# Stick breaking by pairs of heads, gate jobs spread over the linear attention's scan, and a stage of four branch splits dissolved

## What is computed

```python
# branch 2: stick breaking, 8 heads of 64, by blocks of 128 queries
z = einsum("bhqd,bhkd->bhqk", q * 64 ** -0.5, k)
log_keep = where(strict, log_sigmoid(-z), 0)
between = cumsum(log_keep, axis=3, reverse=True) - log_keep
weights = where(strict, exp(log_sigmoid(z) + between), 0)
y_c = einsum("bhqk,bhkd->bhqd", weights, v)
# branch 3: gated linear attention, 4 heads of 128, chunks of 16 tokens
#   o = q_dec @ state + (causal q_dec k_inv^T) @ v;  state = state * g_last + k_dec^T @ v
y_d = rms_norm(o) * silu(gate)
# merge
gates = sigmoid(x @ w_merge)                   # 4 x 1024 columns
merged = sum(gates[n] * (y[n] @ w_branch[n]) for n in range(4))
out = merged @ w_out
```

## Time and profile before

| | us |
|---|---|
| runs | 1879.58, 1874.11, 1877.41 |
| median | 1877.41 |
| profiled execution | 1880.32 |
| its span | 1878.5 |
| TensorE busy | 1638.3 (87%) |
| VectorE busy | 1237.1 (66%) |
| ScalarE busy | 826.8 (44%) |
| mean granted clock | 0.926 |

### The profile page before, as it was taken

The page is one execution under the profiler, slowest core; times in us unless marked ns, Lnnn a source line. Parts: engine busy times, 40 slices in busy tenths (PEclk is TensorE's granted clock), DMA queues, the critical chain, the costliest instruction groups (busy, mean ns, idle before and its releaser), DMA issues. The chain is left out here.

```text
span 1878.5 us, 25694 instructions
## 1 busy us (share of the span) xinstructions
PE 1638.3 (87%) x10701; PEld 1477.9 (79%) x10701; DVE 1237.1 (66%) x1389; ACT 826.8 (44%) x953; POOL 33.0 (2%) x48
## 2 busy tenths in 40 slices
PE   2899998999799997999979996887896938999994
PEld 2789887999698987999868996766785837888883
DVE  4777488778657556665455956435564747899895
ACT  1345434333334543344234562236613316777772
POOL 0100000000100000000000000000000000000000
PEclk9999999999899998999989998978887968999997
DMA  8964347898654234566265552102311336999991
GB/s 300 301 220 158 135 138 255 305 320 301 208 149 135 92 111 147 179 228 220 69 178 167 177 159 68 44 25 67 91 67 62 118 136 228 364 350 368 361 342 68
DMA packets 226041, 348.07 MB, mean 185 GB/s; under 512 B 14596, under 2 KB 156656, under 8 KB 225792
## 3 DMA queue, kind: packets, MB, share of 16 engines
q1 hardware_dynamic: 225920, 346.36, 54.9%
HBM read 345.29 MB, written 1.97 MB: 185 GB/s over the span
## 5 line engine op out<-in xcount | busy, mean ns | idle before, releaser
L457 PE MATMUL bank<-layer_split,hT_pair 128*128 128x256 f32 (+1 forms) x4224 | 513.4, 282 | 9.6 <-DVE hT_pair L314 4.6
L457 PEld LDWEIGHTS bank<-layer_split,hT_pair 128*128 128x128 f32 x4224 | 499.3, 191 | 15.7 <-issue 9.0
L184 DVE TENSOR_TENSOR layer_split<-layer_raw,layer_split 128x2048 fp32r<-128x2048 f32 x122 | 279.6, 2292 | 98.6 <-ACT layer_split L172 97.1
L172 ACT ACTIVATE layer_split<-layer_raw 128x2048 fp32r<-128x2048 f32 x122 | 233.7, 1915 | 203.6 <-PE bank L457 114.2
L184 DVE TENSOR_TENSOR expert_split<-expert_raw,expert_split 128x2048 fp32r<-128x2048 f32 x96 | 219.4, 2289 | 41.5 <-ACT expert_split L172 41.3
L172 ACT ACTIVATE expert_split<-expert_raw 128x2048 fp32r<-128x2048 f32 x96 | 184.2, 1920 | 71.5 <-PE bank L1782 39.5
L457 PE MATMUL bank<-split_w,hT_pair 128*128 128x256 f32 (+1 forms) x1248 | 179.8, 308 | 31.5 <-PEq L599 13.7
L457 PEld LDWEIGHTS bank<-split_w,hT_pair 128*128 128x128 f32 x1248 | 170.2, 204 | 42.2 <-issue 34.9
L184 DVE TENSOR_TENSOR split_w<-raw_w,split_w 128x2048 fp32r<-128x2048 f32 x52 | 119.2, 2292 | 52.8 <-ACT split_w L172 52.3
L669 PE MATMUL bank<-layer_split,ffnh_aT 128*128 128x512 f32 x528 | 127.0, 396 | 2.8 <-DVE ffnh_aT L741 2.8
L172 ACT ACTIVATE split_w<-raw_w 128x2048 fp32r<-128x2048 f32 x52 | 99.4, 1912 | 62.1 <-PE bank L457 52.8
(11 more groups left out here) (447 smaller groups left out, 1828.6 us busy)
## 6 DMA issues: line engine op xcount, KB each, us to landing
layer_raw<-in_ada_w SPq DMA_DIRECT2D x48, 1024.0 KB, 5.7
layer_raw<-in_ffn_w_gate_up SPq DMA_DIRECT2D x44, 1024.0 KB, 5.2
raw_w<-in_w_in SPq DMA_DIRECT2D x40, 1024.0 KB, 5.1
layer_raw<-in_w_in SPq DMA_DIRECT2D x38, 1024.0 KB, 6.6
expert_raw<-in_w_gate SPq DMA_DIRECT2D x32, 1024.0 KB, 7.3
expert_raw<-in_w_up SPq DMA_DIRECT2D x32, 1024.0 KB, 7.2
expert_raw<-in_w_down SPq DMA_DIRECT2D x32, 1024.0 KB, 7.0
layer_raw<-in_ffn_w_down SPq DMA_DIRECT2D x22, 1024.0 KB, 5.1
```

The costliest lines, as they stand in the source:

```text
L172: self.nc.scalar.activation(self.pair[:, j % self.pairs, 0, 0:self.size[n]], self.raw[:, n % self.depth, 0:self.size[n]], ACT.Copy).then_i ...
L184: self.nc.vector.tensor_tensor(self.pair[:, j % self.pairs, 1, 0:self.size[n]], self.raw[:, n % self.depth, 0:self.size[n]], self.pair[:, ...
L457: ins = nc.tensor.matmul(out, lhs, rhs, start=c == 0 and tp + wp == 0, stop=c == job.k - 1 and tp == 1)
```

## The change

Four edits.

1. `stick_breaking` goes over 4 pairs of heads. The buffers hold two heads (temps of twice the size), and every elementwise instruction that can do so takes both: minimum, Exp, Ln, maximum and add, the middle part of `keep`, Exp of the weights. Those that read a bank (one a head), the strict parts of `keep` and the masks are one a head, the latter over two blocks of 128 columns at once. TensorE has one gate job after the scores and one after the cumulative products of a round. The low half of a unit comes every round, ahead of `keep`.
2. `gla` gets its 12 jobs in another order over the 16 steps.
3. `gla` also splits branches 0 and 1: two ScalarE copies at steps 12 and 14 (the first waits until all gate jobs have used `hP`), two VectorE subtractions after the state scan of head 3 and two steps later.
4. The four `split_fm` calls go. `LateSplit` splits branches 2 and 3 at the head of the merge's block, and the jobs of these branches wait for it.

```diff
@@ project
+                        if job.wait is not None:
+                            pe.wait_ge(*job.wait)
@@ LateSplit
+            def wait(self, n):
+                return (self.lo_done.sem, n - 1) if n >= 2 else None
+            def scalar(self, act):
+                self.ring.hi(act, self.first)
+                for row, pair in zip(self.rows, self.pairs):
+                    signal(nc.scalar.activation(pair[:, 0, :, :].rearrange("p c s -> p (c s)"),
+                                                row[:, :, :].rearrange("p c s -> p (c s)"), ACT.Copy), self.hi_done)
+                self.ring.hi(act, self.ring.ahead(self.first, 1))
+            def vector(self, dve):
+                self.ring.lo(dve, self.first)
+                for n, (row, pair) in enumerate(zip(self.rows, self.pairs)):
+                    dve.wait_ge(self.hi_done.sem, n + 1)
+                    signal(nc.vector.tensor_tensor(pair[:, 1, :, :], row[:, :, :], pair[:, 0, :, :].bitcast(FP), ALU.subtract),
+                           self.lo_done)
+                self.ring.lo(dve, self.ring.ahead(self.first, 1))
@@ mixer
-                for n in range(4):
-                    split_fm(f"mixer_split{n}", yT[n], yP[n], 4)
+                split = LateSplit(ring, U_BR, yT[2:4], yP[2:4])
-                project("mixer_merge", ring, jobs)
+                project("mixer_merge", ring, jobs, norm=split)
@@ stick_breaking, TensorE
+                    for i in range(PAIRS + 2):
+                        if i < PAIRS:
+                            if i >= 1:
+                                pe.wait_ge(scaled.sem, 2 * i)
+                            for h in range(2):
...
+                            ins.then_inc(scored, 1)
                             beside.multiply(pe, 1)
+                        if 1 <= i <= PAIRS:
+                            n = i - 1
+                            pe.wait_ge(kept.sem, 3 * n + 3)
+                            if n >= 1:
+                                pe.wait_ge(added.sem, 2 * n)
+                            for h in range(2):
...
+                            ins.then_inc(cumed, 1)
+                            beside.multiply(pe, 1)
+                        if i >= 2:
+                            n = i - 2
+                            pe.wait_ge(masked.sem, 2 * n + 2)
...
@@ stick_breaking, VectorE
+                            for h in range(2):
+                                signal(v.tensor_tensor(wt[:, n % 2, h, :], score[:, n % 2, h, :], ps[2 + h][:, 0:Wd], ALU.add), added)
+                        ring.lo(dve, min(first + i + 1, ring.ahead(last, 1)))
+                        if i < PAIRS:
+                            dve.wait_ge(logged.sem, i + 1)
+                            kp, lg = keep[:, i % 2, :, :], ab[:, i % 2, :, :]
+                            done(dve, v.scalar_tensor_tensor(lg, score[:, i % 2, :, :], 0.0, lg, ALU.max, ALU.add), floored)
+                            for h in range(2):
+                                signal(v.scalar_tensor_tensor(ends(kp[:, h, :]), ends(lg[:, h, :]), -1.0, strict, ALU.mult, ALU.mult), kept)
+                            signal(v.tensor_scalar(kp[:, :, P:S], lg[:, :, P:S], -1.0, None, ALU.mult), kept)
@@ stick_breaking, ScalarE
+                    for i in range(PAIRS + 1):
+                        if i < PAIRS:
+                            act.wait_ge(prepped.sem, i + 1)
+                            z = ab[:, i % 2, :, :].rearrange("p h s -> p (h s)")
+                            done(act, a.activation(z, z, ACT.Exp), exped)
+                            signal(a.activation(z, z, ACT.Ln, bias=1.0), logged)
+                        if i >= 1:
+                            act.wait_ge(added.sem, 2 * i)
+                            w = wt[:, (i - 1) % 2, :, :].rearrange("p h s -> p (h s)")
+                            signal(a.activation(w, w, ACT.Exp), weighed)
+                        beside.leave(act, True, 2 * i)
+                        ring.hi(act, min(first + i + 1, ring.ahead(last, 1)))
+                        beside.leave(act, True, 2 * i + 1)
@@ gla, ScalarE
                 for h in range(4):
                     yield
+                    if h >= 2:
+                        if h == 2:
+                            act.wait_ge(ring.used, ring.uses(beside.jobs[-1].unit))
+                        signal(a.activation(hP[:, 0, 4 * (h - 2):4 * (h - 2) + 4, :].rearrange(flat),
+                                            early[h - 2][:, :, :].rearrange(flat), ACT.Copy), early_hi)
                     act.wait_ge(o_sum, h + 1)
@@ gla, VectorE, after the state scan of head h (h up to 4)
+                    if h >= 3:
+                        dve.wait_ge(early_hi.sem, h - 2)
+                        pair = hP[:, :, 4 * (h - 3):4 * (h - 3) + 4, :]
+                        signal(v.tensor_tensor(pair[:, 1, :, :], early[h - 3][:, :, :], pair[:, 0, :, :].bitcast(FP), ALU.subtract),
+                               early_lo)
                     yield
@@ gla
-            woven(ring, beside, [2, 2, 2, 2, 2, 1] + [0, 1] + [0] * 8, {"tensor": tensor, "scalar": scalar, "vector": vector})
+            woven(ring, beside, [2, 1, 1, 1, 1, 1] + [1, 1, 1, 1, 1] + [0] * 5, {"tensor": tensor, "scalar": scalar, "vector": vector})
```

More of the change, by code:

```diff
@@ L1473, in _, with __init__, tensor, gpsimd @@
                                               ps[b][:, :]).then_inc(out, 1)
+        class LateSplit:
+            def __init__(self, ring, first, rows, pairs):
+                self.ring, self.first, self.rows, self.pairs = ring, first, rows, pairs
+                self.hi_done, self.lo_done = Count(nc, "late_split_hi"), Count(nc, "late_split_lo")
+            def wait(self, n):
+                return (self.lo_done.sem, n - 1) if n >= 2 else None
+            def tensor(self, pe):
+                pass
+            def gpsimd(self, pool):
+                pass
+            def scalar(self, act):
[11 more added lines that the diff above has]
+                self.ring.lo(dve, self.ring.ahead(self.first, 1))
+            def ready(self, pe, c):
+                pass
         def second_part():
@@ new lines, in stick_breaking @@
+            Wd, PAIRS = S + P, 4
+            ab, score, keep, wt = (temps[:, i, :, :].rearrange("p b (h s) -> p b h s", h=2) for i in range(4))
+            scored, cumed, mixed = (new_sem(nc, f"sb_pe_{n}") for n in ("scored", "cumed", "mixed"))
+            scaled, prepped, floored, kept, added, masked, out = (
+                Count(nc, f"sb_dve_{n}") for n in ("scaled", "prepped", "floored", "kept", "added", "masked", "out"))
+            exped, logged, weighed = (Count(nc, f"sb_act_{n}") for n in ("exp", "log", "weights"))
@@ new lines, in stick_breaking, with ends, _ @@
+            first = beside.jobs[0].unit
+            last = beside.jobs[-1].unit
+            def ends(z):
+                return z.rearrange("p (c s) -> p c s", c=3)[:, 0:3:2, :]
+            strict = const("sb_strict").unsqueeze(1).broadcast_to([P, 2, P])
+            with nc.Block() as block:
+                @block.sync
+                def _(sp):
+                    ring.feed(sp, ring.ahead(last, 1))
+                @block.tensor
+                def _(pe):
+                    for i in range(PAIRS + 2):
[3 more added lines that the diff above has]
+                            for h in range(2):
+                                kk, qq = k[64 * h:64 * h + 64, i, :], q[64 * h:64 * h + 64, i, :]
+                                nc.tensor.matmul(ps[h][:, 0:S], kk[:, 0:P], qq, start=True, stop=True)
+                                ins = nc.tensor.matmul(ps[h][:, S:Wd], kk[:, P:S], qq[:, P:S], start=True, stop=True)
+                            ins.then_inc(scored, 1)
+                            beside.multiply(pe, 1)
+                        if 1 <= i <= PAIRS:
[4 more added lines that the diff above has]
+                            for h in range(2):
+                                kp, bank = keep[:, n % 2, h, :], ps[2 + h]
@@ L2720, in _ @@
-                    @block.scalar
-                    def _(act):
-                        for i in range(H + 1):
-                            if i < H:
-                                act.wait_ge(prepped.sem, i + 1)
-                                z = ab[:, i % 2, :]
-                                done(act, a.activation(z, z, ACT.Exp), exped)
-                                a.activation(z, z, ACT.Ln, bias=1.0).then_inc(logged.sem, 1)
-                            if i >= 1:
-                                n = i - 1
-                                act.wait_ge(added.sem, n + 1)
-                                w = wt[:, n % 2, :]
-                                a.activation(w, w, ACT.Exp).then_inc(expd.sem, 1)
-                            beside.leave(act, True, i)
-                            ring.hi(act, min(first + i // 2 + 1, first + n_beside))
-                        beside.leave(act, True, len(beside.jobs))
@@ L2739, in gla @@
```

(1 more changed line is left out.)

127 lines of the change are left out of this document (39 added, 88 removed).

## The result

| | before | after |
|---|---|---|
| median | 1876.62 (4 runs, 1874.11 to 1879.58) | 1855.35 (4 runs, 1844.37 to 1861.75) |
| ratio | | 0.9873, 95% interval 0.9845 to 0.9902 |
| profiled execution | 1880.32 (span 1878.5) | 1844.37 (span 1842.5) |

The account below looks back on a forecast made before the run. No engine fills stick breaking, linear attention or norm; TensorE's clock is partly low, and everything later waits for the mixer. Terms 2 + 11 + 4 + 8.6 - 0.2 = 25.4 us gave 1854.9 or 1852.0; 1854 named, range 1848 to 1867.

Parts of the forecast that it names:

- The sum itself: Whole kernel: gains of stick breaking, front, scan and splits, less 0.2 us, together 25.4 us.
- its two results: Whole kernel: 1854.9 us counted from the profiled execution, 1852.0 counted from the median of three runs.
- Stick breaking, forecast 69.5 us: Stick-breaking stage by pairs of heads: rounds of 15.2 us, 2 us less than 71.5; bounds -4.5 to +6.
- Rival B: Stick breaking doesn't gain, as every round pauses TensorE: stage 75 to 77 us, kernel 1860; chance 0.13.
- The front, forecast 11.0 us earlier: Linear attention up to first state products: fewer jobs ahead, so these start 11.0 us earlier; bounds 9 to 12.
- The scan, forecast 37.1 us: First state products to last output: 4 us less than 41.1, with TensorE the bound at the high clock.
- rival A: Scan: TensorE falls to 1.2 GHz again behind the last gate job, 6.4 us back, kernel 1860; chance 0.19.
- The bound for this term: Scan: 63 us if all its jobs, updates and outputs run at the low clock.
- the prediction's own sign: Scan: the prediction is wrong if this stretch is above 41 us.
- The splits, forecast 8.6: Stage splitting four branches: its 9.1 us go but for a 0.5 us hand-over, 8.6 us less; bounds 7.5 to 9.
- The cover in the merge: Merge: second unit ready 6.4 us after the start, asked for at 7.7, so 1.3 us to spare.
- Rivals C and D: C: low clock in both stages, 1902 us, chance 0.04. D: table switches cost more than their load, 1863, chance 0.02.

Follow-up runs that it names:

- r4: The changed kernel with VectorE's low half of the next gate unit last in a round of stick breaking, not ahead of `keep`: 1840.41 us, ratio 0.9793.
- r1: The changed kernel with the old order of the 12 gate jobs in the linear attention: 1861.19 us, ratio 0.9918.
- r0: The changed kernel again, no edit: 1856.0 us, ratio 0.988 to the kernel before.
- r2: The changed kernel with the old stick breaking, head by head: 1863.71 us, ratio 0.9925.
- r3: The changed kernel with the four splits back in a stage of their own ahead of the merge: 1864.37 us, ratio 0.9925.
- r8: The kernel of r4 again, unedited, on another chip: 1838.35 us, ratio 0.9782.
- r9: The kernel of r4 with one unused product of 256 columns ahead of each 8 narrow instructions in the scan: 1841.04 us, ratio 0.9791.
- r5: The changed kernel with the last gate job moved later, behind the outputs of head 2: 1857.58 us, ratio 0.9877.
- r6: The changed kernel with jobs 8 to 11 in one block behind the updates of head 1: 1868.12 us, ratio 0.9927.
- r10: The changed kernel without the 60 narrow products of a chunk with its state, so it does less work: 1844.24 us.
- r11: The kernel of r4 with the old order of the gate jobs: 1845.86 us, ratio 0.982.

## Why the prediction was right, and where it was not

**The time** came within 1.4 us of the forecast by the median (1855.35 against 1854). That closeness is luck in part. Two errors cancel in the sum: stick breaking brings 5.7 us more than its term (7.7 against 2), and the job order 9.8 less (5.2 against 11 + 4). The sum itself was 25.4 us, 4.1 more than the medians show; 1854 was picked between its two results.

**Stick breaking, forecast 69.5 us, took 64.2 to 64.7.** The chain that was added up is the right one: VectorE to ScalarE to the low half to `kept`, in that order and with 8 table loads ahead of jobs. Rounds were 14.2 and 14.5 us against 15.2, and the first scores cost 1.7 us against 3. Behind the last round's `keep` stood 9.1 us against 10.5, as two pairs of value products took 1.6 and not 3.2. The error is the sum's sizes. In the rounds, instructions of one engine in a row overlap, which adding their durations counts twice. In the front the second Exp starts at 1337.76, though the first, at 1336.80, lasts 1.06: 0.10 us of overlap. The two masks took 0.75 against 0.84, the `kept` instructions 0.96 against 1.15 (1276.56 to 1277.52). The Trainium skill (ScalarE: Activation LUTs, What ACT_TABLE_LOAD costs) puts the overlap of ACTIVATEs in a row at about 93 ns, and the trace agrees. Rival B, a stage of 75 to 77, didn't occur: TensorE did pause in every round, and the job behind the scores paid for it (4.54 and 4.63), but the job behind the cumulative products ran at 3.1.

What the step overlooked matters more. Its sum did hold what the low half waits for: from the Ln to the maximum it counts a load, Exp, Tanh, high half and low half, 6.7 us, and the row shows 6.5. But it names the low half ahead of `keep` as the one thing that moves onto the chain, at its own 2.29 us, and never asks what the chain would be without it. By r4, taking it off the chain is worth 14 us in this stage (64.6 to 50.3), as its wait for ScalarE and the pauses of TensorE behind it go too. What moved onto the chain was a wait, not only an instruction. The pairs could have brought 21 us, not 7.

**The front, forecast 11.0 us earlier, is exactly that** (43.9 to 32.9, and 43.9 again in r1). The step read in the earlier trace rows, that ScalarE's emptying and split stand ahead of the Exp for `eb`, is what made it late.

**The scan, forecast 37.1 us, failed.** This is the term that the prediction called its largest uncertain one: jobs at 2.9 and outputs at 4.0, at the high price throughout. In the first profile it took 40.4, with the last head's outputs at 6.42: rival A, at half its size, since in before two heads paid that price. In r0, r2 and r3 it took 48.0, since jobs behind the state products of head 1 and behind outputs cost 5.4 us. The bound for this term was 63 us with all at the low level, so 48 was inside; but no rival had the middle case, jobs at the low price between the outputs, and it is the common one. By the prediction's own sign, a scan above 41 us, this step is wrong. The spread of the runs fits it: the first profile with 40.4 is of a run at 1844, the one of r0 with 48.0 of a run at 1859 (6.3 of these 14.5 us lie ahead of stick breaking). The gain of the front is thus real, and most of it is given back behind it.

**The splits, forecast 8.6, brought 8.7** in the traces and 8.4 by the medians. The early copies and subtractions cost nothing: the second subtraction ends at 1385.96, and the last outputs at 1388.63. The cover in the merge was 1.3 us, as forecast.

**Rivals C and D** are out. The scan's clock didn't fall below 0.70 but rose. After a load the Exp starts within 1.3 us. The rule of the Trainium skill (ScalarE: Activation LUTs, What ACT_TABLE_LOAD costs), 2.66 us a switch, isn't borne out here: at 1269.11 a load begins, at 1270.41 its ACTIVATE.

**Open.** Why one execution grants the high clock in the scan and another doesn't, at the same instructions. The first of the jobs in question is the one behind the state products of head 1. It was fast in all three profiles of kernels with the low half last and the jobs spread (r4, r8, r9). Of the seven other profiles with that job in that place it was fast in one (after) and slow in six (r0, r2, r3, r5, r6, r10). The level at which the scan begins doesn't decide: the granted clock is 1.00 in all ten profiles from ahead of the first state products up to the start of those of head 1. In the slow ones it falls about 2 us later, inside them (at 1362.0 in r0), and there they take 3.87 to 3.99 us; in the fast ones they take 3.04. What does separate the ten is where the clock last rose: 15.0 to 15.2 us ahead of the state products of head 1 in the six slow profiles, 15.6 to 15.8 in after, r4 and r9, and 9.1 in r8. So half a microsecond between the program and the clock's changes goes with 7 us of scan. This was read from the rows afterwards; no run moves the one against the other, so that it decides isn't shown. r11 speaks against the low half's place as what decides: if the low half last made the scan take 40.4 in all of r4's runs, the old order should have cost some 10 us, and it cost 5.4 to 7.5.

## What to carry to other kernels

Moving filler work into a stretch is worth what it removes in front less what it costs behind, at the price that the clock gives there; take both prices from the trace and, where the instructions around the filler are narrow or wait, make the low one a case of its own with its chance. When an instruction moves ahead of another on an in-order engine, price the wait that it carries (what it waits for, and who waits behind it), not its duration alone, and add up the chain with it elsewhere too: here 2.3 us of work were 14 us of stage. And compare stages of more than one profiled execution before telling a gain from luck: here 14 us separated two profiles of one kernel.

## What the runs showed of the chip that was not expected

The granted clock can stay low while TensorE has work all the time: in r0's scan it is busy for 47.24 of 48.0 us at 0.75. A run of 30 instructions of 16 columns has the clock down for the job behind it in some executions (5.47 us in r0) and not in others (3.10 in after, same order). Without these products the two jobs behind outputs cost 3.1 each in the one profile (r10), and one product of 256 columns ahead of each 8 of the instructions didn't keep the clock up (r9). The Trainium skill (TensorE: Matmul & The Clock Gate, The HAM clock gate) has the clock follow how busy the engine was of late; if busy is read as the profile's busy time, r0's row does not agree. That busy time includes products that are narrow or that follow VectorE bank by bank.

The state products of head 1 took 3.04 us at a granted clock of 1.00 (after), since they follow VectorE's scan, and 3.87 to 3.99 where the clock fell inside them; those of head 0, right behind a job, took 1.17. A run of instructions that is long in a row isn't by that alone at the low clock.
